# Differential attention with whole-unit score banks, spread context units and second turns one unit later

## What is computed

```
s_m  = (q_m @ k_m^T) * 64**-0.5          m = 0, 1; keys: 256 of the context, then 512 of the sequence
p    = softmax(s_0) - lam * softmax(s_1)  softmax in float32 over all keys
y    = p @ v                              then a norm over the head's 128 values
```

## Time and profile before

| what | value |
|---|---|
| median of three runs | 4229.64 us |
| the profiled execution | 4231.93 us, its span 4230.1 us |
| busy share of the span | PE 94%, DVE 40%, ACT 24%, POOL 19% |
| stage `differences`, layer 0 | 1885.85 to 1980.13 us |
| stage `differences`, layer 1 | 3358.26 to 3430.82 us |
| mean granted TensorE clock | 0.984 of full speed |

### The profile page before, as it was taken

The page is one execution under the profiler, slowest core; times in us unless marked ns, Lnnn a source line. Parts: engine busy times, 40 slices in busy tenths (PEclk is TensorE's granted clock), DMA queues, the critical chain, the costliest instruction groups (busy, mean ns, idle before and its releaser), DMA issues. The chain is left out here.

```text
span 4230.1 us, 65478 instructions
## 1 busy us (share of the span) xinstructions
PE 3996.5 (94%) x28448; PEld 2713.6 (64%) x28448; DVE 1671.5 (40%) x2600; ACT 1035.7 (24%) x2175; POOL 812.5 (19%) x640
## 2 busy tenths in 40 slices
PE   8999999999999999998999799999899999979888
PEld 6788889887888767566555443333576778833332
DVE  2585854374444342627434300000436464421102
ACT  2212521222111221516211321111314252221111
POOL 2100022113442021113233101000131234400000
PEclk9999999999999999999999899999999999989999
DMA  3584300122223212010112399999320102389997
GB/s 112 205 285 147 89 18 4 44 100 74 80 87 95 68 56 87 6 60 1 60 60 100 130 379 389 387 388 366 106 87 26 60 21 100 120 339 427 427 427 307
DMA packets 194195, 668.89 MB, mean 158 GB/s; under 512 B 11751, under 2 KB 75943, under 8 KB 169335
## 3 DMA queue, kind: packets, MB, share of 16 engines
q1 hardware_dynamic: 188022, 644.01, 40.3%
q0 software_dynamic: 5888, 20.70, 1.6%
HBM read 642.52 MB, written 22.15 MB: 157 GB/s over the span
## 5 line engine op out<-in xcount | busy, mean ns | idle before, releaser
L555 PE MATMUL psum<-arena 128*128 128x264 f32 (+2 forms) x7120 | 1781.8, 412 | 13.5 <-DVE arena L610 3.7
L555 PEld LDWEIGHTS psum<-arena 128*128 128x128 f32 x7120 | 1349.5, 190 | 439.5 <-issue 11.8
L1444 PE MATMUL psum<-arena 128*64 128x512 f32 x3072 | 697.6, 601 | 43.7 <-DMA arena<-in_w_e 39.3
L1444 PEld LDWEIGHTS psum<-arena 128*64 128x64 f32 x3072 | 211.9, 137 | 466.4 <-issue 425.4
L590 ACT ACTIVATE arena<-psum 128x256 f32<-128x256 f32 (+2 forms) x405 | 169.4, 418 | 925.9 <-PE psum L555 871.5
L454 POOL TENSOR_TENSOR arena<-arena 128x512 f32<-128x512 f32 (+1 forms) x114 | 160.1, 1405 | 1025.0 <-PE psum L555 964.8
L2406 DVE TENSOR_TENSOR arena<-arena,psum 128x512 f32<-128x512 f32 x32 | 22.0, 688 | 786.6 <-PE psum L1452 532.5
L382 PE MATMUL psum<-arena 128*128 128x265 f32 (+2 forms) x1120 | 256.1, 387 | 3.3 <-ACT arena L3110 3.3
L382 PEld LDWEIGHTS psum<-arena 128*128 128x128 f32 (+1 forms) x1120 | 208.9, 188 | 42.8 <-ACT arena L3110 3.7
L2860 PE MATMUL psum<-arena 64*64 64x64 f32 x7424 | 225.9, 220 | 8.4 <-issue 4.5
L2860 PEld LDWEIGHTS psum<-arena 64*64 64x64 f32 x7424 | 224.1, 135 | 11.4 <-issue 8.6
(11 more groups left out here) (415 smaller groups left out, 3967.6 us busy)
## 6 DMA issues: line engine op xcount, KB each, us to landing
arena<-in_w_e SPq DMA_DIRECT2D x192, 2048.0 KB, 12.3
arena<-in_w_in SPq DMA_DIRECT2D x38, 2048.0 KB, 8.0
arena<-in_w_ada SPq DMA_DIRECT2D x24, 2048.0 KB, 8.4
arena<-in_ffn_up SPq DMA_DIRECT2D x22, 1024.0 KB, 7.5
arena<-in_w_branch SPq DMA_DIRECT2D x6, 2048.0 KB, 7.8
arena<-in_ffn_down SPq DMA_DIRECT2D x8, 1408.0 KB, 7.9
arena<-in_w_in SPq DMA_DIRECT2D x16, 512.0 KB, 4.5
arena<-in_w_out SPq DMA_DIRECT2D x4, 2048.0 KB, 8.3
```

The lines of the kernel that those rows point to most:

```text
L555: mm = pe.matmul(PS[:, bank, 0:cn], loaded, moved, start=fresh and k == 0, stop=k == h - 1, skip_group_check=not fresh)
L1444: mm = pe.matmul(PS[c * HD:c * HD + HD, b + (m > 0), :], x(kk), w[:, k, c * BW:c * BW + BW], start=(kk == 0), stop=(kk == KT - 1))
```

## The change

It has four parts.

1. The scores of a unit take three banks: even units banks 0 to 2, odd units banks 3 to 5. A full unit's first map has the first 768 values of its 1536 and the second map the last 768, so the two share the middle bank. The pieces are now 512 and 256 keys: map 0 the first 512, map 1 the first 256, map 1 the last 512, map 0 the last 256. The last piece waits (`da_apart`) until the second has ended, since both write the middle bank. `scores(n)` waits for both exponentials of unit n-2. Both exponentials wait for both maxima of their unit.
2. In layer 0 each head's units are ordered context, two full, context, two full.
3. GpSimd scales the first map by its reciprocal, as soon as the first exponential's sum is there. VectorE takes the reciprocals one at a time, multiplies the second by minus `lam`, and its last product scales the second map and adds the first.
4. TensorE's order in a round is scores(n), turn(n-3, 1), gather(n-3), turn(n-2, 0). ScalarE's order is rearranged: power(n, 0), take_turned(n-2, 1), power(n, 1), take_out(n-2), take_turned(n-1, 0).

```diff
@@ attention_units
         for h in range(DA_H):
-            da += [(h, True, q) for q in q_ctx] + [(h, False, CTX + n * P) for n in range(SEQ // P)]
+            full = [(h, False, CTX + n * P) for n in range(SEQ // P)]
+            half = len(full) // 2
+            da += [(h, True, q) for q in q_ctx[:1]] + full[:half] + [(h, True, q) for q in q_ctx[1:]] + full[half:]
@@ layer
-        DA_BANK = lambda n, m: (2 * n + m) % 3 * 2
+        score_banks = PS[:, 0:6, :].rearrange("p b t -> p (b t)")
+        def da_scores(n, m, k0, kn):
+            c = (3 * (n % 2) + 2 * m) * BANK if da[n][1] else 3 * (n % 2) * BANK + m * T2
+            return score_banks[:, c + k0:c + k0 + kn]
@@ TensorE, scores(n)
-                    if n:
-                        wt(pe, "da_e", 2 * n - 1)
-                    cn = CTX if own else T2 // 2
-                    for c in range(1 if own else 2):
-                        for m in range(2):
...
+                    if n >= 2:
+                        wt(pe, "da_e", 2 * n - 2)
+                    split = T2 - BANK
+                    pieces = [(0, 0, CTX), (1, 0, CTX)] if own else \
+                        [(0, 0, BANK), (1, 0, split), (1, split, BANK), (0, BANK, split)]
+                    for m, k0, kn in pieces:
+                        r = slice(m * HD, m * HD + HD)
+                        if (m, k0) == (0, BANK):
+                            wt(pe, "da_apart", n_full[n])
...
+                        if not own and (m, k0) == (1, 0):
+                            inc(mm, "da_apart")
@@ TensorE, the rounds
                 for n in range(len(da) + 3):
                     if n < len(da):
                         scores(n)
+                    if n >= 3:
+                        if not da[n - 3][1]:
+                            turn(n - 3, 1)
+                        gather(n - 3)
                     if 2 <= n < len(da) + 2:
                         turn(n - 2, 0)
-                    if n >= 3:
-                        gather(n - 3)
-                    if 2 <= n < len(da) + 2 and not da[n - 2][1]:
-                        turn(n - 2, 1)
@@ ScalarE
                 def power(n, m):
-                    wt(act, "da_max", 2 * n + m + 1)
+                    wt(act, "da_max", 2 * n + 2)
...
-                for n in range(len(da) + 3):
-                    if 2 <= n < len(da) + 2:
-                        take_turned(n - 2, 0)
+                for n in range(len(da) + 2):
                     if n < len(da):
                         power(n, 0)
-                    if 2 <= n < len(da) + 2 and not da[n - 2][1]:
+                    if n >= 2 and not da[n - 2][1]:
                         take_turned(n - 2, 1)
-                    if n >= 3:
-                        take_out(n - 3)
                     if n < len(da):
                         power(n, 1)
+                    if n >= 2:
+                        take_out(n - 2)
+                    if 1 <= n < len(da) + 1:
+                        take_turned(n - 1, 0)
@@ GpSimd
-                x1 = at(DA_S(n, 1), DA_KEYS(n))
-                wt(pool, "da_r", n + 1)
-                inc(nc.gpsimd.tensor_scalar(x1, x1, at(cell(n, 2) + 1, 1), at(LAMC, 1), ALU.mult, ALU.mult), "da_x1")
+                x0 = at(DA_S(n, 0), DA_KEYS(n))
+                wt(pool, "da_r0", n + 1)
+                inc(nc.gpsimd.tensor_scalar(x0, x0, at(cell(n, 2), 1), None, ALU.mult), "da_x0")
@@ VectorE
-                def inverse(n):
-                    wt(dve, "da_e", 2 * n + 2)
-                    inc(V.reciprocal(at(cell(n, 2), 2), at(cell(n, 1), 2)), "da_r")
+                def first_inverse(n):
+                    wt(dve, "da_e", 2 * n + 1)
+                    inc(V.reciprocal(at(cell(n, 2), 1), at(cell(n, 1), 1)), "da_r0")
                 def normal(n):
...
-                    wt(dve, "da_x1", n + 1)
-                    inc(V.scalar_tensor_tensor(out=x, in0=x, scalar=at(cell(n, 2), 1), in1=x1, op0=ALU.mult,
-                                               op1=ALU.subtract), "da_p")
+                    c = at(cell(n, 2) + 1, 1)
+                    wt(dve, "da_e", 2 * n + 2)
+                    step(V.reciprocal(c, at(cell(n, 1) + 1, 1)))
+                    step.done()
+                    step(V.tensor_scalar(c, c, at(LAMC, 1), -1.0, ALU.mult, ALU.mult))
+                    step.done()
+                    wt(dve, "da_x0", n + 1)
+                    inc(V.scalar_tensor_tensor(out=x, in0=x1, scalar=c, in1=x, op0=ALU.mult, op1=ALU.add), "da_p")
```

More of the change, by code:

```diff
@@ L777, in wt @@
         eng.wait_ge(S(name), v + base.get(name, 0))
-    def spread(ap, n):
-        return ap.rearrange("p (c n) -> p c n", c=n)
     def layer_scalars(step, l):
@@ L1222, in scores @@
                         wt(pe, "rope_t", 8)
-                    if n:
-                        wt(pe, "da_e", 2 * n - 1)
-                    cn = CTX if own else T2 // 2
-                    for c in range(1 if own else 2):
-                        for m in range(2):
-                            r = slice(m * HD, m * HD + HD)
-                            mm = pe.matmul(PS[:, DA_BANK(n, m) + c, 0:cn], A[r, QR + h * T2 + q:QR + h * T2 + q + P],
-                                           A[r, KR + h * T2 + c * cn:KR + h * T2 + c * cn + cn], start=True, stop=True)
+                    if n >= 2:
[7 more added lines that the diff above has]
+                            wt(pe, "da_apart", n_full[n])
+                        mm = pe.matmul(da_scores(n, m, k0, kn), A[r, QR + h * T2 + q:QR + h * T2 + q + P],
+                                       A[r, KR + h * T2 + k0:KR + h * T2 + k0 + kn], start=True, stop=True)
+                        if not own and (m, k0) == (1, 0):
+                            inc(mm, "da_apart")
                     inc(mm, "da_s")
@@ L1647, in power @@
                         wt(act, "da_t2", n_full[n - 3])
-                    x, b = at(DA_S(n, m), DA_KEYS(n)), DA_BANK(n, m)
-                    src = PS[:, b, 0:CTX] if da[n][1] else PS[:, b:b + 2, 0:T2 // 2]
-                    inc(nc.scalar.activation(x if da[n][1] else spread(x, 2), src, ACT.Exp, bias=at(cell(n, 0) + m, 1),
+                    inc(nc.scalar.activation(at(DA_S(n, m), DA_KEYS(n)), da_scores(n, m, 0, DA_KEYS(n)), ACT.Exp, bias=at(cell(n, 0) + m, 1),
                                              accum_out=at(cell(n, 1) + m, 1)), "da_e")
@@ L2135, in largest @@
                     wt(dve, "da_s", n + 1)
-                    b = DA_BANK(n, m)
-                    src = PS[:, b, 0:CTX] if da[n][1] else PS[:, b:b + 2, 0:T2 // 2]
-                    inc(V.tensor_reduce(at(cell(n, 0) + m, 1), src, AX.X if da[n][1] else AX.XY, ALU.max, negate=True), "da_max")
-                def inverse(n):
-                    wt(dve, "da_e", 2 * n + 2)
-                    inc(V.reciprocal(at(cell(n, 2), 2), at(cell(n, 1), 2)), "da_r")
+                    inc(V.tensor_reduce(at(cell(n, 0) + m, 1), da_scores(n, m, 0, DA_KEYS(n)), AX.X, ALU.max, negate=True), "da_max")
+                def first_inverse(n):
+                    wt(dve, "da_e", 2 * n + 1)
+                    inc(V.reciprocal(at(cell(n, 2), 1), at(cell(n, 1), 1)), "da_r0")
                 def normal(n):
                     x, x1 = (at(DA_S(n, m), DA_KEYS(n)) for m in range(2))
-                    wt(dve, "da_x1", n + 1)
-                    inc(V.scalar_tensor_tensor(out=x, in0=x, scalar=at(cell(n, 2), 1), in1=x1, op0=ALU.mult,
-                                               op1=ALU.subtract), "da_p")
+                    c = at(cell(n, 2) + 1, 1)
[6 more added lines that the diff above has]
+                    inc(V.scalar_tensor_tensor(out=x, in0=x1, scalar=c, in1=x, op0=ALU.mult, op1=ALU.add), "da_p")
                 for n in range(len(da) + 1):
@@ L2153, in differences @@
                     if n:
-                        inverse(n - 1)
+                        first_inverse(n - 1)
                     if n < len(da):
```

## The result

| kernel | median (range, runs) | against before, 95% interval |
|---|---|---|
| before | 4229.99 us (4227.66 to 4231.15, 4) | |
| changed | 4257.91 us (4255.83 to 4258.47, 4) | 1.0064 [1.0049, 1.0079] |

The forecast was 4243.4 us in a range of 4234 to 4254, with 0.83 on slower. The sign was right; the step is +27.9 us instead of +13.8, and the time lies outside the range. The profiled execution took 4257.64 us with a span of 4255.8.

What follows compares the result with a forecast made beforehand. The prediction took TensorE, busy 94% of the span, as the bound. Layer 1 +9.6, layer 0 +3.3 and score pieces +0.9 gave +13.8 us: 4245.7 for the profiled execution, 4243.4 as the forecast median, range 4234 to 4254.

Steps and rivals of the forecast that it cites:

- The second part of the turns: Before each gather TensorE waits for ScalarE's copy of turn part 1: 0.80 us a full unit, +8.8 in layer 1's middle.
- The end of layer 1: Behind layer 1's last scores, three units drain with their copies uncovered: 15.1 us against 11.93, so +3.2.
- its start: Layer 1 up to its fifth scores: three banks with two units in flight shorten the filling by 2.4 us.
- Four unequal score pieces: In the score blocks, the last piece's bank wait is hidden by little: +0.03 us a unit, +0.9 for 28 units.
- Rival 1: Score pieces run in strict program order: +0.43 us a unit, 4255; half if only the bank wait shows, 4249. Chance 0.12.
- POOL scales the first map: GpSimd's earlier scaling and VectorE's added 0.3 us a unit were costed at nothing; without cover, 8 us.
- Layer 0, context units apart: Layer 0's heads: new unit order gains 1.8 us, copies cost 3.2, a middle head 22.4 against 21.01; layer 0 +3.3.
- the half-rate stretches: Stretches at half clock rate, such as 2.3 us at layer 1's start, were taken as equal in both kernels.
- rival 4: New TensorE waits bring a half-rate clock stretch in each of five more heads: +11.5 us, 4255. Chance 0.05.
- Rival 2: The copy before the gather costs nothing, lying inside waits for exponentials: -12.8 us, 4217, faster. Chance 0.05.
- Rival 3: Within 0.2%: copy at its lower bound 0.58 us and half-rate stretches gone: +3, 4233. Chance 0.10.

Runs made afterwards that it cites:

- the other first piece: Changed kernel with the second map's piece of 256 keys issued first, ahead of the first map's 512; 4246.8 us, ratio to before 1.0033.
- the fast product: Changed kernel with GpSimd's product written with two operations (times the reciprocal, then times 1.0) instead of one; 4251.8 us, ratio to before 1.0043.
- the three faults: Taken out of the changed kernel together: rounds of before, two-operation GpSimd product, second map's 256 keys issued first; 4223.1 us, ratio to before 0.9979.

## Why the prediction was right or wrong

**The second part of the turns: right.** Forecast 0.80 a unit, measured 0.75, through the wait named: transposes, copy, gather. The end of layer 1 (3.2 forecast, 3.5 measured) and its start (-2.4, -2.0) follow the same working; in layer 1, 10.0 with its share of the pieces was forecast and 11.5 came. That the eleven units came as near as +10.1 to +8.8 is in part luck. The prediction read the unit of 3.81 as free of waits, but 0.17 of it was one, for the exponential of the unit before, which the banks took away; this offset about half of what it had missed in the pieces (0.75 + 0.33 - 0.17 = 0.91 a unit). At the end the copies of part 0 stand uncovered as laid out:

```profile
3449.84 0.60 PE L1252 MATMUL psum<-arena 128*128 128x128 f32 x4
3451.12 0.44 PE L1252 MATMUL psum<-arena 128*128 128x128 f32 x2 [0.69 <-ACT arena L1666]
3452.08 1.58 PE L1263 MATMUL psum<-arena 128*128 128x128 f32 x12 [0.52 <-issue]
```

**"Four unequal score pieces": the step that failed most.** It took the end of the second piece's two passes, at about 0.8, as the time at which the last piece is released, under the first map's stream. The passes do run side by side, as it said: the block with the other first piece is 1.49. But the report of the second piece comes with the end of the 512-column piece ahead of it in the program, and the last piece's weights load only then, 1.19 after the block's start. The term was 0.33 a unit instead of 0.03: 9.2 us instead of 0.9, and 11 by the medians. Rival 1 put half of its price to the bank wait alone and gave 4249 for it.

Starts do not keep the program's order. In the changed kernel, of the passes of one block that TensorE has begun by 3390.29, one is of the first piece of 512 columns and two are of the second, of 256:

```profile
L1237 PE MATMUL psum<-arena x3: 376/480/693, 3389.8 to 3390.1; 64*128 64x256 f32 x2, 64*128 64x512 f32 x1
```

Counted as rival 1 counts, with starts in program order, the order of the experiment would take 0.215 + 3 x 0.43 = 1.5 and 0.2 of starting (an estimate from the prediction's figures for the passes); it takes 1.49. Of the Trainium skill's rule in "TensorE: Matmul & The Clock Gate", "Part 3: Packing small matmuls", that matmuls start and end in program order, the half on starts does not agree with these traces, and the half on ends agrees with when the second piece is seen as done. The prediction set the whole rule aside for the half that fails.

**"POOL scales the first map": wrong, costed at nothing.** It counted VectorE's new instructions, which are indeed hidden, and let GpSimd's product pass as the one of before. The form it has in the change stands in no row of before. Bounded from both sides, as the other terms were, it would have had a term. It was 2.20 us against 0.98, worth some 6 us by the medians in this change (3.6 in the traces), 24 alone.

These two are the steps that put the time outside the range: the pieces' 9.2 less the 0.9, and 6.1 for the product, on top of 13.8 are 28.2. That this all but equals the measured 27.9 is in part luck again, since the vanished wait of 0.17 (some -5 us) and the 2.1 us outside the stages stand in no term.

**Layer 0, context units apart: wrong in what is waited for.** The forecast was 0.35 of waiting for exponentials twice a head and a gain of 1.8 a head from the new order. In the changed kernel TensorE waits there for VectorE's difference instead, 0.58 twice a head, behind the slow product. With the fast product the wait for exponentials is there as laid out, but it is 0.62 and not 0.35. So the place and the number of waits were right, the size and, in this kernel, the releaser were not. With three banks and the rounds of before, the old order of the units has shorter heads; with the new rounds it was not tried. A head was 23.49 instead of 22.4: 4 x 0.33 = +1.3 for the pieces, 2 x 0.58 - 0.7 = +0.5 for the waits, and 4 x 0.22 = -0.9 for the copy at 0.75 and the vanished wait of 0.17, together 23.3.

**The sum of what was found.** By medians: the banks and the rest without the three faults -9.2 (4223.1 against 4232.3 for before on the same chips), the copy +15.6 (4238.8), and from there to the changed kernel's 4257.9 +19.1 for the product and the pieces. This last step is what is left over, not a measurement: one at a time the two are 6.1 and 11.1, and with these the sum is +23.6 of the 27.9. They are differences between runs on several chips.

**The clock.** The forecast took the half-rate stretches as equal. In the changed kernel's execution the first stretch of layer 0 has a granted clock of 0.80 instead of 0.85 and the last one 0.95 instead of 1.00. Worked out from these rows, the clock took (1 - 0.80) x 25.26 = 5.1 us from the first instead of 0.15 x 23.13 = 3.5, and 0.05 x 34.13 = 1.7 from the last instead of none, so at most 3.3 of layer 0's +12.1 (an estimate). How much of it the change itself brought stays open, since places and lengths of these stretches differ between executions; rival 4's repetition in every head did not come in the changed kernel, but it did with the old rounds and the slow product.

**Rivals 2 and 3** fell: the copy lies on the path in all full units of layer 1. Rival 2's ground holds only in part, and only in layer 0, where the copy costs 4.1 us in 16 full units. Rival 3 needed the copy at its lower bound of 0.58, and it is 0.75.

## What to carry over

A copy between two dependent steps of one engine must have other work of that engine between them, and the price of taking that work away can be worked out beforehand: here to 0.05 us a unit. When an edit writes an instruction in another form, a missing operation or another kind of operand, its time is unknown, however much it looks like the old one; measure it alone. Where a matmul must wait for an earlier matmul, put the one it waits for ahead of longer ones in the program: in these runs its report waited for theirs.

## Not expected of the hardware

- GpSimd's float32 tensor-scalar with a per-partition scalar takes 2.20 us on 128 x 768 with one operation and 0.91 with a second one by the constant 1.0 (0.98 with two per-partition scalars); on 128 x 256 it is 0.92, 0.48 and 0.55. Why is not known.
- Two-pass float32 matmuls on different halves of the rows stream side by side, yet one is seen as done only after those ahead of it in the program: 0.33 us a unit, gone when two pieces change places.
- In the kernel with the old rounds and the slow product, six of layer 0's waits of 2.2 us for VectorE were each followed by a stretch of half clock; the waits of 0.5 to 0.6 in the changed kernel's middle were not.
